# Rows instead of columns for the first block's scalings, a turned router, and GpSimd's weighing put later

## The reference, cut to what matters

```python
# first block, the end of it
mix = einsum('btd,de->bte', merged, w_out)
h = h + rmsnorm(mix, post_mix_norm)           # y = x * rsqrt(mean(x^2) + 1e-6) * g
n2 = rmsnorm(h, pre_mlp_norm)
u = square(relu(n2 @ w_up))                   # 1024 -> 4096
h = h + rmsnorm(u @ w_down, post_mlp_norm)    # 4096 -> 1024
# second block, per layer (0: short convolution, dense MLP; 1: block attention, mixture of experts)
x = layer_norm(2**0.5 * x + mix, ln1_g, ln1_b)
ffn = swiglu(x) if layer == 0 else moe_swiglu(x)
x = layer_norm(2**0.5 * x + ffn, ln2_g, ln2_b)
# moe_swiglu
logits = x @ w_router                         # 8 experts
top_logits, top_idx = top_k(logits, 2); top_gates = softmax(top_logits)
out = sum over e of gates[..., e:e+1] * swiglu(x, w_gu[e], w_down[e])
```

## Time and profile before

| what | value |
|---|---|
| runs (median) | 1950.85 us |
| profiled execution, and its span | 1949.0 us, 1947.2 us |
| TensorE busy, share of the span | 95% |
| VectorE, ScalarE, GpSimd | 72%, 55%, 8% |
| mean granted TensorE clock | 0.965 |
| HBM read | 434.99 MB, mean 224 GB/s |

### The profile page before, as it was taken

How to read it: one execution, slowest core, us unless ns; L and a number is a source line. 1 busy time by engine, 2 the same in 40 slices (tenths; PEclk the granted TensorE clock), 3 DMA queues, 4 the chain that set the end, 5 groups by cost and what they waited for, 6 DMA issues and landing times.

```text
span 1947.2 us, 28187 instructions
## 1 busy us (share of the span) xinstructions
PE 1850.9 (95%) x12146; PEld 1690.6 (87%) x12146; DVE 1402.5 (72%) x1600; ACT 1077.0 (55%) x1179; POOL 162.5 (8%) x153
## 2 busy tenths in 40 slices
PE   7899988999999899899989889999999999999997
PEld 6899987998999899899988778888888888888885
DVE  5796376566665465755475578898888889888886
ACT  6653333535554344444333457777767777776774
POOL 0353142001000010100021020000000000000000
PEclk9999989999999998899989779999999999999998
DMA  8232223354555553455545139998999899989993
GB/s 267 87 119 67 87 87 108 132 194 145 164 189 175 172 173 110 159 198 173 189 147 195 41 126 370 374 365 323 368 360 369 320 369 358 369 319 367 360 368 133
DMA packets 278365, 437.95 MB, mean 225 GB/s; under 512 B 10229, under 2 KB 171592, under 8 KB 278104
## 3 DMA queue, kind: packets, MB, share of 16 engines
q1 hardware_dynamic: 278232, 436.07, 64.0%
HBM read 434.99 MB, written 1.05 MB: 224 GB/s over the span
## 4 chain that ended last, share of the span: by engine, by line
PE 82%; DVE 7%; ACT 2%; POOL 1%; issue 1%; DVEq 0%; ACTq 0%; POOLq 0%
PE bank L427 24%; PE bank L429 24%; PE bank L428 24%; DVE ring_r L417 1%; PE bank L2823 1%; PE bank L2334 1%; PE bank L2770 1%; PE bank L1792 1%; ACT hi_ring L402 1%; DVE arena L2249 1%; PE bank L1345 1%; PE bank L1337 1%; PE bank L506 1%; ACT arena L2355 0%; POOL arena L1584 0%
## 5 line engine op out<-in xcount | busy, mean ns | idle before, releaser
L417 DVE TENSOR_TENSOR ring_r<-ring,hi_ring 128x2048 fp32r<-128x2048 f32 (+1 forms) x404 | 912.4, 2285 | 277.5 <-ACT hi_ring L402 277.2
L402 ACT CAST hi_ring<-ring 128x2048 fp32r<-128x2048 f32 (+1 forms) x407 | 763.1, 1904 | 135.1 <-PE bank L429 134.6
L427 PE MATMUL bank<-hi_ring,arena_r 128*128 128x512 f32 (+1 forms) x1456 | 525.1, 361 | 1.5 <-DVE ring_r L417 1.5
L428 PE MATMUL bank<-ring_r,arena_r 128*128 128x512 f32 (+2 forms) x1464 | 522.6, 357 | 0.0
L429 PE MATMUL bank<-hi_ring,arena_r 128*128 128x512 f32 (+1 forms) x1456 | 520.8, 358 | 0.0
L427 PE MATMUL bank<-ring_r,hi_ring 128*128 128x256 f32 (+1 forms) x1400 | 405.6, 290 | 16.4 <-DVE ring_r L538 10.4
L428 PE MATMUL bank<-ring_r,hi_ring 128*128 128x256 f32 (+1 forms) x1400 | 400.9, 286 | 0.0
L429 PE MATMUL bank<-ring_r 128*128 128x256 f32 (+1 forms) x1400 | 400.8, 286 | 0.0
L427 PEld LDWEIGHTS bank<-hi_ring,arena_r 128*128 128x128 f32 x1456 | 276.0, 190 | 43.5 <-DVE ring_r L417 4.6
L428 PEld LDWEIGHTS bank<-ring_r,arena_r 128*128 128x128 f32 (+1 forms) x1464 | 277.0, 189 | 39.8
L429 PEld LDWEIGHTS bank<-hi_ring,arena_r 128*128 128x128 f32 x1456 | 275.7, 189 | 40.8
(11 more groups left out here) (394 smaller groups left out, 1693.1 us busy)
## 6 DMA issues: line engine op xcount, KB each, us to landing
ring<-in_w_gu_moe SPq DMA_DIRECT2D x176, 1024.0 KB, 5.9
ring<-in_w_down_moe SPq DMA_DIRECT2D x88, 1024.0 KB, 5.3
ring<-in_w_in SPq DMA_DIRECT2D x32, 1024.0 KB, 5.2
ring<-in_w_gu_dense SPq DMA_DIRECT2D x22, 1024.0 KB, 5.1
ring<-in_w_up SPq DMA_DIRECT2D x16, 1024.0 KB, 5.4
ring<-in_w_down SPq DMA_DIRECT2D x16, 1024.0 KB, 4.8
ring<-in_w_in_a SPq DMA_DIRECT2D x10, 1024.0 KB, 5.1
ring<-in_w_o SPq DMA_DIRECT2D x8, 1024.0 KB, 4.9
```

The costliest lines, as they stand in the source:

```text
L402: q.e.copy(hi_ring[:, b:b + m], ring[:, a:a + m]).then_inc(*q.did(("hi", of.tag, i)))
L417: q.e.tensor_tensor(ring_r[:, a:a + m], ring[:, a:a + m], hi_ring[:, b:b + m].bitcast(F32), ALU.subtract).then_inc(*q.did(("lo", of.tag, i)))
L427: q.e.matmul(ps, a[0], b[0], start=first, stop=False)
L428: q.e.matmul(ps, a[0], b[1], start=False, stop=False)
```

## The change

1. **mix**. `wo` goes by `pe_tokens`, so its tiles are rows. ScalarE squares each 128 x 256 part with a sum over the free axis (`act_row_squares`), VectorE multiplies by the gain (`dve_row_gains`; the gain is loaded once as rows by a DMA, `sp_gain`). The memory input is turned in the middle of `wo`. Roots and reciprocals are of 128 x 1, the residual is added in rows (`dve_rows_normed`), `n2` is turned by 16 transposes (`pe_norm`) after the memory products of layer 0, and weighed and split like the norms of block two. The 16 tallies and the transposes of `x` go.
2. **mlp**. `mlp_dn` goes by `pe_deep_rows`; the same row scalings, then 16 transposes; X is split straight from PSUM, two k at a time. The 8 tallies, GpSimd's part and the 16 transposes in layer0 go.
3. **GpSimd** weighs the rows of the norms a0 and b0 only after the last split: `pool_norm` waits for `("x", ln, 7)`.
4. **layer1 and router**. `yT` is weighed by ScalarE (k = 0, 1, 4, 5) and VectorE (2, 3, 6, 7). The rows for the picks and for `acc` are turned back from `yT` (16 transposes) and split by ScalarE and VectorE from PSUM; no row weighing and no GpSimd there. The router's 8 columns are stationary and 256 tokens move: 8 matmuls, a copy of 8 x 256, two small transposes. `gap` is computed earlier. One DMA of gains goes.

```diff
     def pe_mix(q):
         for r in range(4):
-            pe_linear(q, "wo", r, "wo", mg, 0, SEQ, lambda k: [("mg", k)], lagging(q, "mix", lambda k: sq_mix[k % 4], SEQ))
-        q.wait_ge(("in", "mem"))
-        pe_turned(q, "memT", memin)
-        pe_tally(q, "mix", lambda k: sq_mix[k % 4], SEQ, 7)
-        q.wait_ge(("in", "x2"))
-        pe_turned(q, "x2", xin2)
+            for c in range(2):
+                pe_tokens(q, "wo", r, "wo", mg, lambda k: [("mg", k)], c)
+            if r == 1:
+                q.wait_ge(("in", "mem"))
+                pe_turned(q, "memT", memin)
         pe_memory(q, 0, "k")
         pe_memory(q, 0, "v")
-        for k in range(8):
-            pe_tally(q, "x2", lambda k: sq_x2[k % 4], SEQ, k)
+        pe_norm(q, "x2", n2)
         pe_memory(q, 1, "k")
         pe_memory(q, 1, "v")
...
+    def act_row_squares(q, name, r, c, junk, sums):
+        q.wait_ge(("ps", name, 2 * r + c))
+        q.e.activation(junk, B(name, 2 * r + c)[:, 0:256], ACT.Square, accum_out=sums[:, c, r:r + 1]).then_inc(*q.did(("rowsq", name, r, c)))
+        q.wait_ge(("rowsq", name, r, c))
+    def dve_row_gains(q, name, r, c, dst, gain):
+        part = slice(256 * r, 256 * r + 256)
+        q.wait_ge(("rowsq", name, r, c), ("in", "gain", name))
+        q.e.tensor_tensor(dst[:, c, part], B(name, 2 * r + c)[:, 0:256], gain[:, part], ALU.mult).then_inc(*q.did(("rowg", name, r, c)))
+    def dve_rows_normed(q, name, c, src, sums, root, more, event):
+        dve_row_sum(q, name, c, sums, root)
+        dve_row_inverse(q, name, c, root)
+        q.wait_ge(("rowg", name, 3, c))
+        for hf in range(2):
+            part = slice(512 * hf, 512 * hf + 512)
+            q.e.scalar_tensor_tensor(out=xr[:, c, part], in0=src[:, c, part], scalar=root[:, c:c + 1], in1=more[:, c, part], op0=ALU.mult, op1=ALU.add).then_inc(*q.did((*event, c, hf)))
...
     def pe_mlp(q):
-        pe_deep(q, "mlp_dn", 32, "mlp_dn", u_, lambda k: [("u", k)], lagging(q, "dn", lambda k: sq_dn[k % 4], SEQ))
-        pe_tally(q, "dn", lambda k: sq_dn[k % 4], SEQ, 7)
+        pe_deep_rows(q, "mlp_dn", 32, "mlp_dn", u_, lambda k: [("u", k)])
+        pe_norm(q, "x3", xr)
...
     def act_mlp(q):
+        for k in range(0, 8, 2):
+            act_split(q, X.hi[:, k:k + 2, :], B("turned", "x3", k).rearrange("p (a t) -> p a t", a=2), ("ps", "turned", "x3", k), ("xhi", "x3", k))
     def dve_mlp(q):
+        for k in range(0, 8, 2):
+            dve_split(q, X.hi[:, k:k + 2, :], X.lo[:, k:k + 2, :], B("turned", "x3", k).rearrange("p (a t) -> p a t", a=2), ("xhi", "x3", k), ("x", "x3", k))
...
     def pool_norm(q, ln):
+        q.wait_ge(("x", ln, 7))
         for c in range(2):
             rows_weighed(q, ln, c)
...
     def pe_layer0(q):
-        for c in range(2):
-            for hf in range(2):
-                ps = B.take(q, "x3rows", c, hf)
-                for k in range(4):
-                    t = q.e.transpose(ps[:, k * P:(k + 1) * P], x2[:, 4 * hf + k, c * P:(c + 1) * P], ident)
-                t.then_inc(*q.did(("ps", "x3rows", c, hf)))
...
     def pe_router(q):
-        two = [B.take(q, "logits", c) for c in range(2)]
+        ps = B.take(q, "logitsT")
         for k in range(8):
             q.wait_ge(ya1(k))
-            for c in range(2):
-                t = q.e.matmul(two[c][:, 0:8], yT[:, k, c * P:(c + 1) * P], wr[:, k, :], start=(k == 0), stop=(k == 7))
+            t = q.e.matmul(ps[0:8, 0:SEQ], wr[:, k, :], yT[:, k, :], start=(k == 0), stop=(k == 7))
+        t.then_inc(*q.did(("ps", "logitsT")))
+        for c in range(2):
+            for hf in range(2):
+                ps = B.take(q, "xt", c, hf)
+                for k in range(4):
+                    t = q.e.transpose(ps[:, k * P:(k + 1) * P], yT[:, 4 * hf + k, c * P:(c + 1) * P], ident)
+                t.then_inc(*q.did(("ps", "xt", c, hf)))
+                if c == 0 and hf == 0:
+                    q.wait_ge(("lgT",))
+                    for a in range(2):
+                        ps = B.take(q, "logits", a)
+                        q.e.transpose(ps[:, 0:8], lgT[0:8, a * P:(a + 1) * P], cc("ident")[0:8, 0:8]).then_inc(*q.did(("ps", "logits", a)))
...
     def act_router(q):
-        for c in (1, 0):
-            act_split(q, xt.hi[:, c, :], xr[:, c, :], ("y", "a1", c), ("xthi", c))
+        for c in range(2):
+            for hf in range(2):
+                part = slice(512 * hf, 512 * hf + 512)
+                act_split(q, xt.hi[:, c, part], B("xt", c, hf), ("ps", "xt", c, hf))
+                q.e.activation(acc[:, c, part], B("xt", c, hf), ACT.Copy, scale=alpha).then_inc(*q.did(("xthi", c, hf), ("acc", "w", c, hf, -1)))
...
-    def pool_router(q):
-        dve_split(q, xt.hi[:, 0, :], xt.lo[:, 0, :], xr[:, 0, :], ("xthi", 0), ("xt", 0))
```

More of the change, by code:

```diff
@@ L499, in pe_tokens @@
         t.then_inc(*q.did(("ps", tile, 2 * g + c), *([("used", W.tag, i)] if c else [])))
[L502 to L530, removed]
     def act_root_ahead(q):
@@ L1985, in dve_memory, with pe_rows, pe_deep_rows @@
             B.drop((("mv", layer), c), ("mv", layer, c))
+    def pe_rows(q, name, tile, x, ready):
+        for r in range(4):
+            for c in range(2):
+                pe_tokens(q, name, r, tile, x, ready, c)
+    def pe_deep_rows(q, name, KT, tile, x, ready):
+        for g in range(4):
+            ps = [B.take(q, tile, 2 * g + c) for c in range(2)]
+            for kb in range(0, KT, 8):
+                i = W.at[name, g, kb]
+                w = halves(i, W)
+                nk = W.blocks[i][1][0]
+                q.wait_ge(("lo", W.tag, i))
+                for c in range(2):
+                    for k in range(nk):
+                        kk = kb + k
+                        q.wait_ge(*ready(kk))
+                        t = mm3(q, ps[c][:, 0:256], (x.hi[:, kk, c * P:(c + 1) * P], x.lo[:, kk, c * P:(c + 1) * P]),
+                                (w.hi[:, k, :], w.lo[:, k, :]), kk == 0, kk == KT - 1)
+                    ends = [("used", W.tag, i)] if c else []
+                    if kb + nk == KT:
+                        t.then_inc(*q.did(("ps", tile, 2 * g + c), *ends))
+                    elif c:
+                        t.then_inc(*q.did(*ends))
@@ new lines, in pe_norm @@
+    def pe_norm(q, ln, src):
+        two = [B.take(q, "turned", ln, k) for k in range(0, 8, 2)]
+        for c in range(2):
+            for hf in range(2):
+                q.wait_ge(("z", ln, c, hf))
+                for k in range(4 * hf, 4 * hf + 4):
+                    a = SEQ * (k % 2) + c * P
+                    t = q.e.transpose(two[k // 2][:, a:a + P], src[:, c, k * P:(k + 1) * P], ident)
+                    if c and k % 2:
+                        t.then_inc(*q.did(("ps", "turned", ln, k - 1)))
@@ L2032, in dve_mix @@
                 q.wait_all("merge")
[L2033 to L2042, removed]
-            q.e.tensor_tensor(x2[:, k, :], tmp_mix[:, k, :], B("x2", k - k % 2)[:, SEQ * (k % 2):SEQ * (k % 2) + SEQ], ALU.add).then_inc(*q.did(("x2", k)))
-            B.drop(("x2", k - k % 2), ("x2", k))
@@ L2056, in dve_mix @@
+        dve_weighed(q, "x2", qx2, range(8), vrows["pre_mlp_norm"])
         dve_memory(q, 1)
@@ L2441, in act_layer0 @@
             act_keep(q, "uc", 2 * r, uc)
[L2442 to L2447 removed]
+        for r in range(3):
             act_high(q, W.at["uh", r] + 2)
@@ L2534, in act_dense @@
         act_norm_roots(q, "b0")
-        act_norm(q, "b0")
+        act_weighed(q, "b0", qt, range(8))
         q.mark("dense")
@@ L2612, in act_layer1 @@
         act_norm_roots(q, "a1")
-        for k in range(8):
+        for k in (0, 1, 4, 5):
             q.wait_ge(("ps", "turned", "a1", k - k % 2))
@@ L2704, in dve_router @@
             q.wait_ge(("m8b", c))
+            q.e.tensor_tensor(gt2[:, c, 2:3], m8b[:, c, 1:2], m8b[:, c, 0:1], ALU.subtract).then_inc(*q.did(("gap", c)))
+        for c in range(2):
             q.e.max_index(ix[:, c, :], m8b[:, c, :], lg[:, c, :]).then_inc(*q.did(("ix", c)))
@@ L3187, in sp @@
                 sp_memory(q)
+            elif i == W.at["mlp_up", 2] + NRAW:
+                q.wait_ge(("end", "mix", "pe"))
+                sp_gain(q, "mlp_dn", "post_mlp_norm", dn_gain)
             elif i == W.at["uc", 0] + NRAW:
```

251 lines of the change are left out of this document (109 added, 142 removed).

## The result

The changed kernel takes 1916.54 us (median of 4 runs, 1912.07 to 1917.74) against 1951.16 us (4 runs, 1948.03 to 1951.74): ratio 0.9815, 95% interval 0.9803 to 0.9827. The profiled execution took 1917.74 us with a span of 1915.8, so within the traces 31.4 us of span are to be explained; the rest is that the profiled execution of before (1949.0 us) was 2.2 us under this median and that of after is 1.2 over its own.

The account below looks back on a forecast made before the run. TensorE's order was taken as the time, so four junctions were added: 9.4 + 9.6 - 2.7 + 1.1 = 17.4 us off 1949.0 gives 1931.6, stated as 1932 for the median; range 1920 to 1942.

Parts of the forecast that it names:

- A: Mix stage: tallies and two waits go, row chains covered by the memory products; gain 9.4 us, bounds 5 to 10.
- B: End of the MLP to layer 0: fewer tallies, shorter chain, 16 transposes gone; gain 9.6 us, bounds 7.5 to 12.
- C: Norms a0 and b0: openings 3.6 us sooner, but GpSimd's late weighing holds ScalarE and TensorE waits; net loss 2.7 us.
- D: Router: rows ready sooner and shorter product, less added copy, transposes and splits; gain 1.1 us, bounds -1 to 3.5.
- (1): Rival at a0 and b0: GpSimd's late weighing is harmless, C gains 7.2 us, time 1922; chance 0.22.
- (2): Rival: row chains in mix and MLP not covered or long; A 5, B 7.5, C -5, D 0, time 1941; chance 0.17.
- (3): Rival: the hold on ScalarE grows, C is -25, time 1954, slower; chance 0.03.
- (4): Rival: the router's swap gains nothing, copy and splits are bare; D -2, time 1935; chance 0.55 together with the forecast.

Follow-up runs that it names:

- f_free: The changed kernel with GpSimd's marks of layer0 and dense set before its weighing, so ScalarE and VectorE don't wait for it: 1905.65 us.
- e_pool: The kernel before with only GpSimd's weighing put behind the last split (change 3): 1946.37 us.
- e_router: The kernel before with only the layer1 and router change (change 4): 1945.97 us.
- f_idle: The changed kernel with eight more VectorE scalings by 1.0, each waiting for the last, at the end of the MLP: 1922.9 us.
- g_best: f_free with the first MLP up block cast and lowered before the last memory tile is copied, in five rounds: 1900.38 us.
- e_first: The kernel before with only the first block's row scalings (changes 1 and 2); router and GpSimd's weighing as before: 1924.49 us.
- g_noswap: The changed kernel with the router's product as before (tokens stationary, 8 columns moving, 16 matmuls), in five rounds: 1920.1 us.

## Why the prediction was wrong

Its direction and its mechanisms held; its size failed by a step that it had hardly priced: **the clock was taken as it was before**. In A it says so ("as before"), in B the clock that stays up is only a bound ("2.2 more"), in C it is only ever a loss. Behind four idle times that shrank, TensorE stayed at 2.4 GHz: at the openings of layer 0 and, mostly, of dense and layer 1, in the whole attention of layer 0, and in the router's product. From the landmarks, the row "opening to the norm of layer 0" alone is 7.9 us beyond its forecast, with the same instructions in it but for the transposes: 2.2 in the opening, 3.9 in the attention (15.4 to 11.5) and 1.8 in the output projection (24.65 to 22.87). From the runs, the mean clock rose from 0.962 to 0.977; 15 steps of 0.9 to 1.16 us are 14 to 17. From the traces, a microsecond at 1.2 GHz cost 0.41 us between the opening and the norm of layer 0 (7.8 us for 19.0) and 0.33 in the attention of layer 1 (a line through the thirteen traces), less than half, in stretches where TensorE also waits (12.1 us busy of the 15.4); the 41 us that the changed kernel has less of them ahead of the experts are then 14 to 17 too, an estimate from these rows. What is left of each part when the mean clock's share is taken off, beside the forecast:

| kernel | mean, to before | of it clock | the rest | forecast |
|---|---|---|---|---|
| parts 1 and 2 (A + B) | -27.9 | -5 to -6 | -22 to -23 | -19.0 |
| part 3 (C) | -4.1 | -6 to -7 | +2 to +3 | +2.7 |
| part 4 (D) | -6.7 | -4 to -5 | -2 to -3 | -1.1 |
| all four | -36.2 | -14 to -17 | -19 to -23 | -17.4 |

(Means of 4, 6, 6 and 9 runs against the 29 of before.) This is a regression and not an experiment: it divides, it doesn't prove. The experiment is the idle put back, where 3.7 us of idle cost 5.6 to 6.4 by the runs and, in the trace, 10.5 up to the norm of layer 0.

The Trainium skill, TensorE: Matmul & The Clock Gate, Part 1, says that for modelling the penalty of the ramp is less than 1% of a typical kernel's span. The 14 to 17 us between these two kernels are 0.7 to 0.9% of 1951, yet nearly half of what this change did. And they are a difference: by the same slopes the whole way from the mean clock of before, 0.962, to full clock, 38 steps, would be 34 to 44 us, 1.8 to 2.3% (an estimate, far outside the clocks that the slopes come from). If all time at the low clock counts as ramp, these runs don't agree with the figure.

Point by point:

- **A** was right: 9.6 for 9.4. The memory products covered the row chains (no wait at 461.02), and the wait of 2.71 and the slow stretch behind it stayed.
- **B** was right in the chain: 8.8 us became 4.4, forecast 4.8. Its end was missed, because the stretch behind it was counted only by its transposes.
- **C** had the mechanism to the instruction: the openings 3.6 and 3.7 sooner, ScalarE released by GpSimd, one VectorE block and one GpSimd instruction taking each other's time. The Trainium skill, SBUF — State Buffer, "Who interferes with whom", gives that as a lock; 4.33 and 3.32 us against 2.4 and 2.29 agree again. The waits came out at 6.1 and 3.0 against some 4 and 2.5, and still the four stretches lost only 1.3 us net (-3.6, +5.4, -3.7, +3.2), forecast 2.7, because the openings kept the clock: the dense stretch took 190.4 us before, with its opening slow, and 188.1 in f_free, at full clock and without a wait. Up to the attention of layer 1, which varies by itself, the loss is 1.0 us. (The sum had a slip of 0.2: 811.0 is 0.7 later than before and was put down as -0.5.)
- **D** was mis-sized, 1.1 for 4.5. In its terms: the product starts 2.7 us sooner behind the row norm (forecast 2.3), takes 3.6 us for 6.83 instead of the 5.5 I chose between 3.6 and 7.2, and from its end to the gather 6.9 us pass instead of 5.8, so the added copy, transposes, subtractions and splits cost 1.1 and not 2.5. The clock's share is the 1.9 us of the product: I had kept the low clock for a product that comes 2.7 us sooner behind a shorter idle.
- **Rivals**: (1), which named 1922, was nearest in number and wrong in cause: the hold is real (the waits of 6.08 and 3.00 are there, and f_free, which lifts it, has neither). (2), (3) and (4) did not come.

The range ended at 1920 since I let the clock add only "two or three" to the best case. A bound of its own, 2.2 us for each of the three openings and 1.9 for the product, would have taken 8.5 off rival (1) and put the low end near 1913.

What stays open: what the runs of e_pool won, since the traced one won nothing; how much of the medians' 3 us is the swap; what sets the clock in the attention of layer 1; why the attention of layer 0 follows the clock of the opening, which the idle put back shows but doesn't explain. The attention began 55.6 to 55.7 us after the clock came back in the opening in the kernel before, in e_pool, e_router and f_idle, and ran slow in all four. Where the opening was at full clock throughout it ran at full clock in seven traces and slow in part in an eighth (g_best); and in e_first, whose opening was slow only from 661.3 to 664.7, it ran at full clock.

## What to carry to other kernels

Where one engine's order is the time, price an idle time at more than its length: look at the granted clock behind it, and ask for each wait that a change shortens or makes whether the stretch behind will be at one level or the other; put that into the sum, with its own bounds. Effects of that kind don't add: a part whose runs are 6 us faster alone can be worth nothing beside the others. And when work is moved off a chain, look at what its completion mark holds up; here moving the mark was worth more (11 us by the medians, 12.6 in the trace) than moving the work. Before two traces are compared as a whole, compare them stretch by stretch, and set apart a stretch that varies by itself.

## What the runs showed of the hardware

- An idle time longer by 3.7 us cost 10.5 us up to the norm of layer 0 in the trace, and 5.6 to 6.4 by the medians of the runs: the 4.4 us behind it ran at 0.50, and so did part of a stretch 60 us on (0.69 over 15.3 us).
- The same attention of layer 1 took 41.3 us in one trace (clock 0.92) and 49.0 in another (0.69).
- Runs of one kernel differ together with their clock: 1911.31 us at 0.981 and 1917.95 at 0.976 for the changed kernel, 1895.12 at 0.984 and 1912.85 at 0.974 for f_free.
- Eight float32 products with 8 columns stationary and 256 moving took 3.61 us at full clock, 0.45 each, the price of the tallies; the other way round, 16 with 8 moving columns took 6.83 at half clock and 4.42 in g_noswap, partly at full clock.
